# Four output chunks turned during the first and third head pair, their products in the fourth, sums behind the row maxima: a two-layer hybrid trunk on one core

## The reference

```python
for l in range(2):                                   # 512 tokens, 1024 features
    h = LN(ALPHA*h + 0.5*swiglu_a(h));  h = LN(ALPHA*h + mixer(h));  h = LN(ALPHA*h + 0.5*swiglu_b(h))
# mixer: proj = h @ w_in, split into
#   6 forgetting heads  : softmax(q k^T/8 + c_q - c_k, causal) @ v                 -> chunks 0,1,2 of y
#   4 differential heads: softmax(s1) - lam*softmax(s2), @ v, rms-normalised, scaled -> chunks 3,4
#   6 spatial gating heads: u * (tril(w_s) @ LN(g) + b_s)                          -> chunks 5,6,7
#   mixer(h) = concat(y) @ w_out
```

## Time and profile before

| | us |
|---|---|
| median of 3 runs | 1911.66 (1911.31 to 1913.45) |
| the profiled execution | 1907.15 |
| its span | 1905.4 |
| PE busy | 1866.6 (98%) |
| VectorE busy | 1412.9 (74%) |
| ScalarE busy | 741.2 (39%) |
| GpSimd busy | 215.8 (11%) |
| granted TensorE clock, mean | 0.999 |

### The profile page before, as it was taken

One profiled execution on the slowest core, in us unless ns is written; L12 is line 12 of the kernel. 1 busy time (PEld: TensorE's weight loads), 2 busy tenths in 40 slices (PEclk: granted clock), 3 DMA queues, 4 the chain that ended last, 5 costly groups with the idle time before them and its releaser, 6 DMA issues.

```text
span 1905.4 us, 25000 instructions
## 1 busy us (share of the span) xinstructions
PE 1866.6 (98%) x9121; PEld 1570.7 (82%) x9121; DVE 1412.9 (74%) x2059; ACT 741.2 (39%) x1114; POOL 215.8 (11%) x247
## 2 busy tenths in 40 slices
PE   7999999999999999999999999999999999999998
PEld 6888888889878888888888888888888888888886
DVE  7887877952666878787897777777536588777778
ACT  5333333435554423333254242333456443424243
POOL 1000000153313000000100000003343220000001
PEclk9999999999999999999999999999999999999999
DMA  6222223245832222222313222223558223222231
GB/s 223 90 110 88 110 88 132 101 127 176 213 93 89 111 88 110 88 110 88 132 70 129 88 110 88 110 110 108 169 144 216 72 71 127 111 88 110 88 110 45
DMA packets 43747, 215.95 MB, mean 113 GB/s; under 512 B 8756, under 2 KB 11252, under 8 KB 20008
## 3 DMA queue, kind: packets, MB, share of 16 engines
q1 hardware_dynamic: 40808, 199.30, 29.6%
q0 software_dynamic: 2880, 15.90, 3.6%
HBM read 197.23 MB, written 17.93 MB: 113 GB/s over the span
## 4 chain that ended last, share of the span: by engine, by line
PE 87%; DVE 6%; issue 2%; ACT 2%; SPq 1%; DMA 1%; POOL 1%; ACTq 0%; DVEq 0%; POOLq 0%
PE psum L997 79%; PE psum L1199 4%; PE psum L1293 1%; DVE res L1518 1%; PE psum L1028 1%; DVE negm L1877 1%; DVE st L1535 1%; PE psum L1283 1%; SPq L445 1%; ACT psum L902 1%; PE psum L1271 1%; DVE xlo L1474 0%; DMA gbc<-in_gb_col 0%; DVE wlam L1894 0%; PE psum L1393 0%
## 5 line engine op out<-in xcount | busy, mean ns | idle before, releaser
L997 PE MATMUL psum<-xhi,whiA 128*128 128x512 f32 (+1 forms) x768 | 286.7, 373 | 5.1 <-DVE xlo L1474 5.1
L997 PE MATMUL psum<-xlo,whiA 128*128 128x512 f32 (+1 forms) x768 | 285.2, 371 | 0.0
L997 PE MATMUL psum<-xhi,wloA 128*128 128x512 f32 (+1 forms) x768 | 285.2, 371 | 0.0
L997 PE MATMUL psum<-xhi,whiB 128*128 128x512 f32 x704 | 274.1, 389 | 0.0
L997 PE MATMUL psum<-xlo,whiB 128*128 128x512 f32 x704 | 274.0, 389 | 0.0
L997 PE MATMUL psum<-xhi,wloB 128*128 128x512 f32 x704 | 274.0, 389 | 0.0
L997 PE MATMUL psum<-whiD,hl 128*128 128x512 f32 x768 | 264.1, 390 | 2.0 <-DVE wloD L1451 2.0
L782 ACT ACTIVATE s<-psum 128x512 f32<-128x512 f32 x40 | 23.9, 598 | 540.7 <-PE psum L997 540.7
L1629 DVE SCALAR_TENSOR_TENSOR res<-psum,res 128x1024 f32<-128x1024 f32 x120 | 146.6, 1222 | 82.2 <-PE psum L997 82.1
L1629 DVE SCALAR_TENSOR_TENSOR nat<-psum,nat 128x1024 f32<-128x1024 f32 x144 | 175.8, 1221 | 26.3 <-PE psum L997 26.3
L997 PEld LDWEIGHTS psum<-xhi,whiA 128*128 128x128 f32 x768 | 144.6, 188 | 32.7 <-DVE xlo L1474 6.0
(11 more groups left out here) (217 smaller groups left out, 3518.9 us busy)
## 6 DMA issues: line engine op xcount, KB each, us to landing
rawA<-in_a_w SPq DMA_DIRECT2D x62, 1024.0 KB, 6.3
rawB<-in_b_w SPq DMA_DIRECT2D x54, 1024.0 KB, 4.8
rawD<-in_d_w SPq DMA_DIRECT2D x46, 1024.0 KB, 4.8
stacks<-hl SPq DMA_DIRECT2D x192, 64.0 KB, 1.7
whiD<-stacks POOLq DMA_DIRECT2D x10, 768.0 KB, 6.0
wloD<-stacks POOLq DMA_DIRECT2D x10, 768.0 KB, 5.8
gbr<-in_gb_row SPq DMA_DIRECT2D x6, 1024.0 KB, 8.4
stacks<-wloD SPq DMA_DIRECT2D x48, 64.0 KB, 1.7
```

The lines of the kernel that those rows point to most:

```text
L997: ins = t_.matmul(out_, a_, b_, start=(start and k == 1), stop=(stop and k == n), skip_group_check=check)
```

## The change

The four early chunks are turned in the first and third pair, one after each of the steps (0,1), (0,5), (2,1), (2,5) (pair index, step), as extra work between two steps, in the bank (6 or 7) that the projection of that pair does not hold at the time. ScalarE and VectorE split each one step later, VectorE behind its row maximum, its `inverse` and its `output`. The parts go to tiles of their own (`hl` 4 to 9 and two thirds of `thi`), since `xhi` is still read. From pair 4 on the slots hold only output products: 16 in pair 4, 12 in pair 5, where the slots 19, 21, 29 and 31 of the 32 stay empty. The first eight products take the two B weights of both tiles and one A weight ahead of the second A weight. The sums (`early_add`) move from the head of a step to behind its row maximum, `inverse` and `output`, ahead of `mix`: steps 3, 4 and 6 of pair 4, and 0, 2 and 5 of pair 5.

```diff
+TURNS = {(0, 1): (0, 7), (0, 5): (2, 6), (2, 1): (3, 7), (2, 5): (1, 6)}
+TURN_AT = list(TURNS)
+FIRST_ITEMS = [(0, 0), (0, 1), (0, 2), (1, 0), (1, 1), (1, 2), (0, 3), (1, 3)]
+EARLY_ITEMS = FIRST_ITEMS + [(u, n) for u in range(2, 8) for n in range(len(EARLY) if u < WHOLE else 2)]
+EARLY_SLOTS = [i for i in range(4 * STEPS) if i not in (19, 21, 29, 31)]
+ADD_STEP = {(EARLY_SLOTS[EARLY_ITEMS.index((u, len(EARLY) - 1))] + 1) // 2: u for u in range(WHOLE)}
...
+        yhi = [hl[:, 4 + i, :] for i in range(4)]
+        ylo = [hl[:, 8, :], hl[:, 9, :], thi[:, 0:S], thi[:, S:2 * S]]
...
 # ScalarE's loop (y_hi), and the same in VectorE's (y_lo)
-                    if b == EARLY_BODY and k < 2:
-                        y_hi(2 * k)
...
-                    if b == EARLY_BODY and k < 2:
-                        y_hi(2 * k + 1)
+                    if (b, k - 1) in TURNS:
+                        y_hi(TURN_AT.index((b, k - 1)))
...
 # PE: project, turn_y, early
+                    turned_before = sum(at < (b - 2, NT * g) for at in TURN_AT)
+                    if turned_before:
+                        pe.wait_ge(yt_ok, l * NC + turned_before)
...
+                    pe.wait_ge(qk_ok, (l * BODIES + at[0] + 1) * 2 + (3 if at[1] > NT else 2))
...
-                for i in range(len(EARLY)):
-                    if i == 1:
-                        pe.wait_ge(qk_ok, (l + 1) * BODIES * 2)
-                    turn_y(l, i)
-                    yield
                 pe.wait_ge(yt_ok, l * NC + len(EARLY))
                 pe.wait_ge(lo_ok["B"], l * B_ALL + B_WO + 1 + AHEAD)
-                for u in range(8):
-                    for n in range(len(EARLY) if u < WHOLE else 2):
-                        if n == 2:
+                for slot in range(4 * STEPS):
+                    if slot in EARLY_SLOTS:
+                        u, n = EARLY_ITEMS[EARLY_SLOTS.index(slot)]
+                        if (u, n) == (0, 2):
+                            pe.wait_ge(qw_ok, (l + 1) * BODIES)
+                        if (u, n) == (0, 3):
                             pe.wait_ge(lo_ok["A"], l * A_ALL + A_WO + 1 + AHEAD)
+                        if (u, n) == (1, 0):
+                            pe.wait_ge(qk_ok, (l + 1) * BODIES * 2)
                         early_output(l, u, n)
-                        yield
+                    yield
...
+                    if (b, k) in TURNS:
+                        turn_y(l, TURN_AT.index((b, k)))
...
 # VectorE's loop
-                    adds = G - EARLY_BODY * STEPS - NT
-                    if adds >= 0 and adds % 2 == 0 and adds // 2 < WHOLE:
-                        early_add(adds // 2)
                     row_max(G)
...
                     if G >= 2:
                         output(G - 2)
+                    if G - EARLY_BODY * STEPS in ADD_STEP:
+                        early_add(ADD_STEP[G - EARLY_BODY * STEPS])
                     if is_diff(G):
                         mix(G)
```

## The result

| | before | after |
|---|---|---|
| median of 6 runs | 1911.61 us (1909.90 to 1913.45) | 1899.43 us (1897.94 to 1900.34) |
| ratio | | 0.9936, interval 0.9924 to 0.9947 |
| the profiled execution | 1907.15 us | 1899.35 us |
| its span | 1905.4 us | 1897.6 us |

The kernel is faster by 12.2 us where 6.4 were predicted; 1899.43 lies 2.9 us under the low end of the range. The direction and the places were right, the size was not. Two differences are to be kept apart from the start: between the *medians* lie 12.2 us, between the two *profiled executions* 7.8.

A forecast was written before the change was run, and what follows sets the result against it. PE, 98% busy, was taken as the bound, so only its waits and work could move the time. Terms summed to -3.4 us a layer, taken as -3.2, -6.4 for both: 1905.3 us, range 1902.3 to 1909.2.

The forecast's parts named there:

- it lay 4.5 under the median of the runs, so the time shown would be 1911.66 - 6.4: Whole kernel: the profiled execution's 4.5 us offset from the median was kept, giving 1905.3 us after a 6.4 us gain.
- turns in pairs 1 and 3: Four turns between steps of pairs 1 and 3 cost PE 0.36 us each, +1.44 us a layer, their waits nothing.
- `y_lo` in step 6 of pair 3: Pair 3, step 6: the later row maximum makes PE's `values` wait for `p_out`, +0.1 us, bounds 0 and 0.9.
- pair 5: Pair 5 with 12 products instead of 16: -3.12 us, less about 0.3 of longer `values` wait in step 4; term -2.8.
- The second count, by waits: One layer counted by waits alone: 0.7 + 2.4 + 0.3 us go, 0.1 + 0.3 come, -3.0 us.
- The queue behind `y_hi` and `y_lo`: VectorE's next row maximum waits behind them, then `exp`, `p_out` and `values`; tightest in step 6 of pair 3, +0.1 us.
- It becomes what pair 2 is: Pair 4 with products in all 16 slots takes pair 2's 22.56 us instead of 24.73, -2.17 us a layer.
- Blocked multiplications: Pair 3, step 6: GpSimd's work drifts back and holds up the `rms` multiplications, 0.7 us more a layer, 1906.8 us; 10%.
- late weights: Pair 4: first products still wait, for the A weights; up to 2 us a layer go, 1909.3 us; 5%.
- row maxima behind the copies: Pairs 1 and 3: copy, subtraction and handing over reach PE at each turn, +3.1 us a layer, 1917.9 us; 5%.
- Pair 5 keeps its length: Pair 5: the chain eats all four products' gain, so a layer gains only 0.6 us, 1910.4 us; 14%.
- a fifth more than the larger count: The range's low end, 1902.3 us, set by a gain a fifth above the larger count of -3.4 us a layer.

The follow-up runs named there:

- the fillers: Kernel before with 18 throwaway matmuls per layer where PE waits for the fourth low part at the head of pair 4; 1908.90 us against 1911.28, ratio 0.9987.
- the wait that was put back: Changed kernel with PE's slot 4 product in pair 4 waiting for the second map's exponentials of the same step; 1904.63 us, ratio to before 0.9958.
- the empty slots first: Changed kernel with its 28 products in slots 4 to 31, so pair 4's first four slots are empty; 1904.72 us against 1911.10, ratio 0.9972.

## Why the prediction was wrong

**The step that failed: "it lay 4.5 under the median of the runs, so the time shown would be 1911.66 - 6.4".** The prediction carried the offset between one execution and the median over as a constant. It was not: before's profiled execution lay 4.5 us under its median, after's 0.1 us under its own (1899.35 against 1899.43). That is 4.4 of the 5.8 us of the miss; the terms of the sum are the rest, and are answered below. In the terms of the mechanism, the prediction priced the wait for `y_lo` at its length and put the fall of the clock behind it at nothing. Two kinds of events lay in the pairs that the change touches, and differ from one execution of before to the next:

- the clock's fall behind the wait for `y_lo`, 1.14 us a layer, in both layers of two of four executions of before. Taken away alone it gives 2.4 us. It is shown by the fillers, and by the wait that was put back. The changed kernel has no such wait, and its profiled execution no fall in the heads.
- the transfer of an A half weight in pair 3 of layer 0. It lengthened the pair by 0.65 to 1.3 us in three of four executions of before (21.68, then 22.33, 22.51, 23.01), while the changed kernel's is 22.50, with its turn. So where before pays for the transfer, the turn may cost little. With the empty slots first the changed order too waited for it (23.34 us). How often it does in the changed kernel was not counted. The same transfer in pair 1 of layer 1 worked against the prediction's execution: with its wait it took 20.04 us, and 19.96 after, with two turns.

Between the heads nothing moved. From the end of layer 0's heads to the start of layer 1's it is 829.01 us before (572.70 to 1401.71) and 829.05 after (569.23 to 1398.28); between executions of before only the start varies too, 460.90 to 462.17 us up to layer 0's heads. After's starts at 461.72, 0.8 us later than that of the prediction's execution, and what follows layer 1's heads took 0.3 us more, so its gain in the heads (8.96 us) shows as 7.8 between the two profiled executions. The four profiled executions of before have a mean of 1909.8 us, 2.7 us over the first: 1.7 of them in the heads, and 0.9 by the start, which the change doesn't touch. Against this mean the change gives 10.5 of the 12.2 us. The other 1.7 us lie in executions that no trace shows; that the plain runs of before have a mean granted clock of 0.997, and the four profiled ones of 0.998, suggests that the clock fell more often in them, but not where; this stays open.

The terms for one layer, against the traces of layer 0:

| term | predicted | measured |
|---|---|---|
| turns in pairs 1 and 3 | +1.44 | +0.85 and +0.82 = +1.67 |
| `y_lo` in step 6 of pair 3 | +0.1 | 0 |
| pair 4 | -2.17 | -2.79 |
| pair 5 | -2.8 | -3.19 |
| sum | -3.4, taken -3.2 | -4.29 (layer 1: -4.67) |

So the heads gave 8.96 us where 6.4 were forecast, with no fall of the clock in either execution. That part of the miss, 2.6 us, is one of mis-sized terms: pairs 4 and 5 gave more, and in layer 1 the turns of pair 1 seem to cost nothing, since before lost the time there to the transfer. The second count, by waits, had -3.0 a layer; the waits in the view fell by 3.5 and 4.1 us (4.4 and 5.0 to 0.9), among them waits of `values` that this count did not include.

**Turns.** In layer 0 0.41 to 0.43 us each instead of 0.36, with no wait for `yt_ok` or `qk_ok`. Right in kind.

**The queue behind `y_hi` and `y_lo`.** Its rows came as worked out: `p_out` is late, the product covers it, and the multiplications run unblocked. In the new timeline `y_lo` waits 0.86 us for ScalarE's copy, and the row maximum is early enough all the same. The margin was thin: `p_out` of that step ends at 527.70, 0.14 us ahead of its `values`, and GpSimd's half weight drifted back 2.5 us (0.8 by the later start of the heads, 0.9 by pair 1's turns, the rest in pair 3), to within 0.7 us of the multiplications. That the subtraction is not held up shows in before: a `y_lo` at 528.36 took its 0.69 us inside GpSimd's 527.92 to 530.28.

**Pair 4.** "It becomes what pair 2 is" was right in its first four steps (10.88 us in pair 2, 10.92 in pair 4) and wrong behind. Pair 2 holds small waits that pair 4 does not. PE's timeline of after, scores of step 4 and the `turn_p` behind them, in pair 2 and in pair 4:

```profile
492.49 0.23 PE L1291 MATMUL psum<-wloD 97*128 97x128 f32 x1
...
494.76 0.66 PE L1303 MATMUL psum<-ident,s 128*128 128x128 f32 x4
```

```profile
537.61 0.23 PE L1291 MATMUL psum<-wloD 97*128 97x128 f32 x1
...
539.46 0.66 PE L1303 MATMUL psum<-ident,s 128*128 128x128 f32 x4
```

2.27 us against 1.85. In pair 2 VectorE's `mix` ends 494.71 and releases it; this and a second such place near the end make the 0.64 us between 22.58 and 21.94. A stretch taken as a yardstick should be looked at for waits below those that the waits view prints.

**Pair 5.** Two errors of opposite sign. The prediction had -3.12 for four products and +0.3 for a longer wait. The sums' new place alone is worth -1.02 in the old layout, as the experiment shows, and the four products the rest by difference, -2.17 (in the new layout, measured by the empty slots first, -2.64): the first wait was gone with the sums, and the fewer products brought back one of 0.75 us in the same step.

**The rivals.** Blocked multiplications, late weights and row maxima behind the copies did not come. "Pair 5 keeps its length" is wrong for pair 5, but its mechanism is there in pair 4, where 12 products take as long as 16. All of them, and both ends of the range, were about the heads of one execution; none asked what the other executions of before did at that wait. The low end, "a fifth more than the larger count", had room for mis-sized terms and none for that; as worded it would even be 1911.66 - 1.2 x 6.8 = 1903.5, not 1902.3.

The Trainium skill (TensorE: Matmul & The Clock Gate, Part 1) says that an idle TensorE falls back to half its clock. The traces agree: the lower level shows behind a wait of 2.4 us, in some executions and not in others. The prediction has no term for the clock. The mean granted clock of its execution, 0.999, was no warning, and could hardly be one: 4 us at 0.57 take less than a thousandth from the mean over 1905 us. Beside the 0.997 of the plain runs it could have been one.

## What to carry to other kernels

A wait of PE can cost more than its length: look at the granted clock in the stretch behind it, and in more than one execution, and compare the mean granted clock of the profiled execution with that of the plain runs. Where the median lies well above the profiled execution, ask which events the others have and whether the change touches their place, before the offset is carried over as a constant. A sum that frees a bank is part of the chain that feeds PE as soon as the products come earlier; move both together.

## What the runs showed of the hardware

- The granted clock fell behind waits of PE of 2.41 and 2.49 us (four of eight layers in four executions of before, and one of two with only the sums moved) and of 1.67 us (one layer with the wait put back). It showed 0.57 to 0.61 in the 4 us behind, and 0.72 and 0.85 in two neighbouring stretches with the sums moved; in stretches of 1 us it is 0.50, the lower level. It did not fall behind waits of 1.88 and 2.12 us in the kernel with the sums at the head of a step, nor behind one of 1.90 us with the wait put back, so the length of the wait alone does not decide. With PE at work in the wait it fell in none of four layers. What decides in a given execution stays open; where it fell in the kernel before, it fell in both layers.
- A fall cost 1.14 us in the kernel before, and 1.57 and 1.58 us with the sums behind the row maxima and with the wait put back (25.27 - 21.94 less 23.94 - 22.19).
- An added 2.35 us of matmuls without use, in a wait, made the kernel 2.4 us faster.
- ScalarE's wait for one transfer varied between 1.10 and 3.05 us from execution to execution with the kernel's order unchanged up to there, and reached PE, in pair 3, with what went beyond 1.63 us. Why the landing varies was not tried.
